# Joined: the experts' last gate and up columns as one product of 512 columns, and attention one's forget gate row among the keys

## The reference

```
s = einsum("bqhd,bkhd->bhqk", qf, kf) * scale                       # 16 heads of 64
s = s + logf_cum[:, :, q0:q1, None] - logf_cum[:, :, None, :q1]     # forget gate, summed over positions
p = softmax(where(mask, s, -inf))

for e in range(8):   # 2816 columns in gate and up
    out = out + gates[..., e:e+1] * (silu(h @ w_gate[e]) * (h @ w_up[e])) @ w_down[e]
```

## Time and profile before

| | |
|---|---|
| median of 3 runs | 1679.54 us (1678.4 to 1681.87) |
| the profiled execution | 1672.49 us |
| its span, first to last instruction | 1670.6 us |
| TensorE busy | 1639.7 us, 98% |
| VectorE busy | 1239.7 us, 74% |
| ScalarE busy | 992.2 us, 59% |
| experts (8 items of some 93.6 us) | about 489 to 1239 us of the span |
| attention one | 405.5 to 444.8 us of the span |

### The profile page before, as it was taken

The page is one execution under the profiler, slowest core; times in us unless marked ns, Lnnn a source line. Parts: engine busy times, 40 slices in busy tenths (PEclk is TensorE's granted clock), DMA queues, the critical chain, the costliest instruction groups (busy, mean ns, idle before and its releaser), DMA issues.

```text
span 1670.6 us, 24525 instructions
## 1 busy us (share of the span) xinstructions
PE 1639.7 (98%) x9456; PEld 1427.2 (85%) x9456; DVE 1239.7 (74%) x1207; ACT 992.2 (59%) x1077; POOL 106.3 (6%) x97
## 2 busy tenths in 40 slices
PE   8999999999999999999999999999999999999998
PEld 6868999898878888888888888888879989979997
DVE  5986544565478988888888898888888478565554
ACT  4245334465457777878787777878774552344443
POOL 1020000000036000000000000000210000000000
PEclk9999999999999999999999999999999999999999
DMA  9405554453059898999989898989994400055450
GB/s 336 154 1 226 190 202 170 158 202 151 25 203 403 312 419 360 391 378 377 422 332 419 332 418 358 395 368 383 373 392 154 152 1 1 8 195 185 175 196 26
DMA packets 53175, 415.17 MB, mean 249 GB/s; under 512 B 6312, under 2 KB 6736, under 8 KB 11888
## 3 DMA queue, kind: packets, MB, share of 16 engines
q1 hardware_dynamic: 49872, 403.65, 61.6%
q0 software_dynamic: 3232, 10.53, 2.0%
HBM read 405.74 MB, written 8.42 MB: 248 GB/s over the span
## 4 chain that ended last, share of the span: by engine, by line
PE 88%; DVE 9%; issue 1%; ACT 1%; DMA 1%; DVEq 0%; SPq 0%; ACTq 0%
PE ps L2040 26%; PE ps L2042 26%; PE ps L2041 26%; DVE big L1816 2%; DVE f L1816 2%; PE ps L2568 1%; PE ps L2376 1%; PE ps L2114 1%; PE ps L2556 1%; DMA ring<-in_ws 1%; PE ps L2495 0%; PE ps L2098 0%; PE ps L2367 0%; PE ps L2128 0%; PE ps L2293 0%
## 5 line engine op out<-in xcount | busy, mean ns | idle before, releaser
L1051 DVE TENSOR_TENSOR wl<-raw,wh 128x2048 fp32r<-128x2048 f32 x194 | 444.3, 2293 | 60.3 <-ACT wh L1046 57.1
L2040 PE MATMUL ps<-wh,f_r 128*128 128x512 f32 (+1 forms) x1216 | 465.3, 383 | 2.0 <-DVE f_r L1782 1.7
L2041 PE MATMUL ps<-wl,f_r 128*128 128x512 f32 (+1 forms) x1216 | 459.8, 378 | 0.0
L2042 PE MATMUL ps<-wh,f_r 128*128 128x512 f32 (+1 forms) x1152 | 435.5, 378 | 0.0
L1046 ACT ACTIVATE wh<-raw 128x2048 fp32r<-128x2048 f32 x192 | 368.3, 1918 | 97.1 <-PE ps L2042 55.0
L2040 PEld LDWEIGHTS ps<-wh,f_r 128*128 128x128 f32 x1216 | 228.8, 188 | 45.0 <-DVE f_r L1782 1.9
L2041 PEld LDWEIGHTS ps<-wl,f_r 128*128 128x128 f32 x1216 | 229.0, 188 | 41.1
L2042 PEld LDWEIGHTS ps<-wh,f_r 128*128 128x128 f32 x1152 | 216.7, 188 | 40.8
L2040 PE MATMUL ps<-ht_t_r,wh 128*128 128x256 f32 x832 | 236.5, 284 | 1.3 <-DVE h_t_r L806 1.0
L2041 PE MATMUL ps<-h_t_r,wh 128*128 128x256 f32 x832 | 235.4, 283 | 0.0
L2042 PE MATMUL ps<-ht_t_r,wl 128*128 128x256 f32 x832 | 235.4, 283 | 0.0
(11 more groups left out here) (446 smaller groups left out, 2137.7 us busy)
## 6 DMA issues: line engine op xcount, KB each, us to landing
raw<-in_ws SPq DMA_DIRECT2D x195, 1024.0 KB, 10.7
raw<-in_ws SPq DMA_DIRECT2D x49, 2048.0 KB, 7.8
big<-in_ws SPq DMA_DIRECT2D x48, 1024.0 KB, 10.9
f<-in_ws SPq DMA_DIRECT2D x24, 1024.0 KB
ring<-in_ws SPq DMA_DIRECT2D x4, 2048.0 KB, 17.9
items<-big SPq DMA_DIRECT2D x8, 512.0 KB, 13.7
gb<-in_gains SPq DMA_DIRECT2D x5, 512.0 KB, 14.2
ring<-in_ws SPq DMA_DIRECT2D x2, 1024.0 KB, 12.8
```

The costliest lines, as they stand in the source:

```text
L1051: nc.vector.tensor_tensor(half_of(wl, h % SPLIT), ring_half(h % HALVES), half_of(wh, h % SPLIT).bitcast(F32), ALU.subtract).then_inc(S("sp ...
L2040: first = nc.tensor.matmul(bank, xh, h, start=start, stop=False)
L2041: nc.tensor.matmul(bank, xh, l, start=False, stop=False)
L2042: return first, nc.tensor.matmul(bank, xl, h, start=False, stop=stop)
```

## The change

**Experts.** The weights of the last step lie on the host as 512 columns, gate's 256 beside up's 256, so a half holds 4 x 512 and not 8 x 256. TensorE makes one product of 512 columns into `ps[1]` from halves 28 and 29, with `transposes(4)` between them. `silu(5)` reads the bank's first 256 columns, `product(5)` multiplies by its last 256. The semaphore `e_gu` counts 11 for an item instead of 12, and ScalarE's `silu(5)` moves behind `tile_t(4)` and half 31.

**Attention one.** The gate's sum becomes one more row of the keys. For an even head the rows 64 to 127 of `KT` are met by zeros in the queries, so row 64 is overwritten by the sum, and the query's row 64 is 1. For an odd head a second copy of the keys, `KTO` (in `g1`), has its own rows 64 to 127 and the sum in row 0, where the odd query has a 1. ScalarE copies the odd keys (four of 64 x 512). GpSimd sets the ones, writes `NL` to a DRAM tensor `decays`, and when this has landed reads it back into the two rows (two DMAs); `g1` is cleared once more after attention. The two matmuls of line 2131, the parts `NLH` and `NLL` and four VectorE instructions that made them are gone, and so is a memset of `NL`.

```diff
@@ gpsimd
             nc.gpsimd.memset(QZS[0], 0.0).then_inc(S("pad"), 1)
+            pool.wait_ge(S("pad"), 3)
+            nc.gpsimd.memset(QZS[0][DH:DH + 1, 0:HEADS:2, :], 1.0).then_inc(S("pad"), 1)
+            nc.gpsimd.memset(QZS[0][0:1, 1:HEADS:2, :], 1.0).then_inc(S("pad"), 1)
+            for n in range(4):
+                b, k = pre.at[("k", n)]
+                pool.wait_ge(pre.free[b], k + 1)
+            pool.wait_ge(S("nl_ready"), 1)
+            pool.dma_start(dr["decays"], NL[0:HEADS, :]).then_inc(S("nl_out"), 16)
+            pool.wait_ge(S("nl_out"), 16)
+            pool.dma_start(KT[DH:DH + 1, :, :], dr["decays"][0:HEADS:2, :].unsqueeze(0)).then_inc(S("nl_rows"), 16)
+            pool.dma_start(KTO[0:1, :, :], dr["decays"][1:HEADS:2, :].unsqueeze(0)).then_inc(S("nl_rows"), 16)
             pool.wait_ge(S("att_done"), 1)
...
+            nc.gpsimd.memset(g1[:, :], 0.0).then_inc(S("pad"), 1)
@@ scalar, keys
             for n in range(4):
                 high_pre(act)
+                b, k = pre.at[("k", n)]
+                act.wait_ge(pre.free[b], k + 1)
+                nc.scalar.activation(KTO[DH:P, 2 * n:2 * n + 2, :], KT[DH:P, 2 * n:2 * n + 2, :], ACT.Copy).then_inc(S("odd_keys"), 1)
@@ scalar, experts
                 high(27, 28, 29, 30)
-                silu(5)
                 tile_t(4)
                 high(31)
+                silu(5)
@@ vector, keys
-            ch(nc.vector.memset(NL, 0.0))
...
-            ch(nc.vector.tensor_tensor_scan(NL[0:HEADS, :], FA[0:HEADS, 3, :], FA[0:HEADS, 1, :], 0.0, ALU.mult, ALU.subtract))
-            ch.go(nc.vector.tensor_copy(NLH[:, 0:SEQ], NL))
-            ch(nc.vector.tensor_copy(NLH[:, SEQ:3 * P], NL[:, 0:P]))
-            nc.vector.tensor_tensor(NLL[:, 0:SEQ], NL, NLH[:, 0:SEQ].bitcast(F32), ALU.subtract).then_inc(S("nl_ready"), 1)
-            nc.vector.tensor_tensor(NLL[:, SEQ:3 * P], NL[:, 0:P], NLH[:, SEQ:3 * P].bitcast(F32), ALU.subtract).then_inc(S("nl_ready"), 1)
+            nc.vector.tensor_tensor_scan(NL[0:HEADS, :], FA[0:HEADS, 3, :], FA[0:HEADS, 1, :], 0.0, ALU.mult,
+                                         ALU.subtract).then_inc(S("nl_ready"), 1)
@@ vector, experts
+                    up = ps[2 + s % 2][:, 0:w] if s < 5 else ps[1][:, w:2 * w]
@@ tensor, attention
-                            pay(nc.tensor.matmul(bank[:, 0:256], qs[:, h, P:2 * P], KT[:, h // 2, 0:256], start=True, stop=False))
-                            nc.tensor.matmul(bank[:, 256:384], qs[:, h, 0:P], KT[:, h // 2, 0:P], start=False, stop=False)
-                            for part in (NLH, NLL):
-                                nc.tensor.matmul(bank[:, 0:384], IDA[:, h:h + 1].to_broadcast([P, P]), part, start=False, stop=False)
+                            keys = (KT, KTO)[h % 2]
+                            pay(nc.tensor.matmul(bank[:, 0:256], qs[:, h, P:2 * P], keys[:, h // 2, 0:256], start=True, stop=False))
+                            nc.tensor.matmul(bank[:, 256:384], qs[:, h, 0:P], keys[:, h // 2, 0:P], start=False, stop=False)
...
-            pe.wait_ge(S("nl_ready"), 2)
+            pe.wait_ge(S("odd_keys"), 4)
+            pe.wait_ge(S("nl_rows"), 32)
@@ tensor, experts
                 for s in range(6):
-                    product(ps[s % 2], 512 if s < 5 else 256)
-                    if s:
-                        transposes(s - 1)
-                    product(ps[2 + s % 2], 512 if s < 5 else 256)
                     if s == 5:
+                        product(ps[1], lambda: transposes(4))
                         rows(0)
                         rows(1)
                         down_step(4, lambda: transposes(5))
-                    elif s:
+                        continue
+                    product(ps[s % 2])
+                    if s:
+                        transposes(s - 1)
+                    product(ps[2 + s % 2])
+                    if s:
                         down_step(s - 1)
```

More of the change, by code:

```diff
@@ L424, in build @@
         IDA, CAU = big_r[:, 2816:2816 + P], big_r[:, 2816 + P:2816 + 2 * P]
-        NLH, NLL = big_r[:, 3072:3072 + 3 * P], big_r[:, 3072 + 3 * P:3072 + 6 * P]
         SUMS = rt[:, 96:128].rearrange("p (t h) -> p t h", t=TT)
         FA = big[:, 1792:1792 + 4 * SEQ].rearrange("p (b s) -> p b s", b=4)
-        KT = f1[:, :].rearrange("p (c s) -> p c s", s=SEQ)
+        KT, KTO = (t[:, :].rearrange("p (c s) -> p c s", s=SEQ) for t in (f1, g1))
         HKBS = [t[:, 1024:2048].rearrange("p (h s) -> p h s", s=SEQ) for t in (f1, f3)]
@@ L1090, in delta_act @@
         def delta_act(act, ch):
-            act.wait_ge(S("pad"), 6)
+            act.wait_ge(S("pad"), 9)
             for n in range(6):
@@ L1261, in _ @@
             norm_act(act, pre, 2, "x_done", 2, [("mix1", HTQ), ("kv", HTK)])
-            act.wait_ge(S("pad"), 3)
+            act.wait_ge(S("pad"), 5)
             high_pre(act)
@@ L1299, in _ @@
             act.wait_ge(S("routed"), 1)
-            act.wait_ge(S("pad"), 5)
+            act.wait_ge(S("pad"), 7)
             act.sem_inc(S("y_out"), 1)
@@ L1306, in silu @@
                     w = 512 if s < 5 else 256
-                    act.wait_ge(S("e_gu"), i * 12 + (2 * s + 1))
+                    act.wait_ge(S("e_gu"), i * 11 + (2 * s + 1))
                     nc.scalar.activation(SG[:, s % 2, 0:w], ps[s % 2][:, 0:w], ACT.Silu).then_inc(S("e_silu"), 1)
@@ L1593, in delta_dve @@
             bank2 = filled(dve, post, ("gT",))
-            dve.wait_ge(S("pad"), 7)
+            dve.wait_ge(S("pad"), 10)
             ch(nc.vector.tensor_copy(GTR, bank2[0:GH, 0:SEQ]))
@@ L1921, in product @@
                     w = 512 if s < 5 else 256
-                    dve.wait_ge(S("e_gu"), i * 12 + (2 * s + 2))
+                    dve.wait_ge(S("e_gu"), i * 11 + min(2 * s + 2, 11))
                     dve.wait_ge(S("e_silu"), i * 6 + (s + 1))
-                    nc.vector.tensor_tensor(PRD[:, s % 2, 0:w], ps[2 + s % 2][:, 0:w], SG[:, s % 2, 0:w],
+                    up = ps[2 + s % 2][:, 0:w] if s < 5 else ps[1][:, w:2 * w]
+                    nc.vector.tensor_tensor(PRD[:, s % 2, 0:w], up, SG[:, s % 2, 0:w],
                                             ALU.mult).then_inc(S("e_prod"), 1)
@@ L2329, in _ @@
             gather(1, None, 2)
-            pe.wait_ge(S("pad"), 5)
+            pe.wait_ge(S("pad"), 7)
             for n in range(4):
@@ L2345, in half_unit, with product @@
                     return half_of(wh, h % SPLIT), half_of(wl, h % SPLIT)
-                def product(bank, n):
-                    per = HALF // n
+                def product(bank, between=None):
+                    n, per = 512, HALF // 512
                     for part in range(DC // per):
+                        if part and between:
+                            between()
                         h, l = (t.rearrange("p (c n) -> p c n", c=per) for t in half_unit())
@@ L2731, in lay_out @@
             else:
-                put(g[:, :, sl], u[:, :, sl])
+                put(np.concatenate([g[:, :, sl], u[:, :, sl]], axis=2))
             if s:
@@ L2785 @@
     dr["scratch"] = nc.dram_tensor("scratch", (GH, HK), F32).ap()
+    dr["decays"] = nc.dram_tensor("decays", (HEADS, SEQ), F32).ap()
     dr["tokens"] = nc.dram_tensor("tokens", (SEQ, D), F32).ap()
```

## The result

The changed kernel takes **1671.3 us** (median of 20 runs, 1665.85 to 1675.03) against 1675.23 for the kernel before on the same chip (20 runs, 1671.61 to 1681.87). The ratio is 0.9969, interval 0.9956 to 0.9982: 0.31% faster, some 5.2 us. That is the distance of the two means. The medians lie only 3.9 us apart, but each list falls into two groups (before: ten runs up to 1673.8 and ten from 1676.7 on), so a median stands in a gap or at its edge and is the looser figure. The three runs of before shown ahead lay high with their 1679.54. The spans of the profiled executions are 1670.6 and 1665.8 us, 4.8 apart.

The account below looks back on a forecast made before the run. TensorE was taken as the bound, nearly gapless in experts and attention one. The experts' 2.4 us plus attention's 3.6 make 6.0 off 1679.54, giving 1673.5 us (ratio 0.9964), range 1669.5 to 1678 us.

Parts of the forecast that it names:

- A pair of matmuls for one is worth 12.5 ns, the step 2.4 us: Experts' last step: 24 wide matmuls replace 48 narrow, 0.30 us an item, 2.4 us over 8 items.
- The rival that wide ones gain nothing: Experts' step: a wide matmul gains almost nothing over two narrow, leaving 3.6 us, 1675.9 us; chance 0.05.
- the 0.5 us by the gap that the Trainium skill gives: Experts' step: by a gap of N/2.4 + 2.5 ns a pair is worth 2.5 ns, the step 0.5 us.
- The later silu costs nothing, a slack of 0.25 stays: Experts' tail: nothing on VectorE waits for `silu(5)`; slack before the last down step falls from 0.40 to 0.25 us.
- The rival of the stalled tail: Experts' tail: the later silu delays VectorE's chain by 0.55 us or more, leaving 3.6, 1675.9 us; chance 0.13.
- 0.35 us a head, heads of 1.77: Attention one: dropping two 384-column matmuls a head saves 0.35 us, 5.6 over 16; heads some 1.77 us up to head 8.
- The first exponentials take back 0.7: Attention's start: three pairs go but ScalarE's answer comes only one pair earlier, so 0.7 us is lost.
- 0.8 and 0.5 are lost in heads 8 to 15, since VectorE is nearly full: Attention: 0.8 us lost from head 8's maxima to head 9's values, 0.5 in heads 13 to 15; 3.6 us left.
- New waits at heads 9, 11 and 13, under 1 us: Attention, next profile: TensorE newly waits for VectorE's copies of these odd heads, under 1 us each.
- The rows cost nothing: GpSimd's two DMA trips, 3 us each, end at 397, ahead of attention at 405.47; slack 8 us.
- The warning about VectorE and GpSimd's descriptors: Rows' DMAs: VectorE can delay GpSimd's descriptor writing, some 0.6 us becoming 3.1; 2.5 more a trip stays inside the slack.
- Everything after each stage only shifts: Whole kernel: work behind the changed stages keeps its length, so the 6.0 us comes off the total.

Follow-up runs that it names:

- e13_later: The changed kernel with VectorE's low part of four finished heads one head later (heads 9, 13, 17 instead of 8, 12, 16); 1666.31 us, one run.
- e5_quarters: The changed kernel with VectorE's two quarters of a weight half moved from behind heads 8 and 10 to behind heads 7 and 13; ratio to before 0.9958.
- e3_again: The changed kernel run once more, unaltered, for a second profile; 1671.14 us, ratio to before 0.9967.
- e6_table: The changed kernel with ScalarE's table of exponentials loaded ahead of attention; 1667.81 us, ratio to before 0.9951.
- e1_attention: The changed kernel with the experts' edits undone, leaving attention's half alone; 1673.08 us, ratio to before 0.9971.
- e8_trips: The changed kernel with the gate's sum written to DRAM seven times instead of once, one behind the other, ahead of the reads; 1672.43 us, one run.
- the fill: Matmuls of no use added in TensorE's last two waits of attention; on the changed kernel alone 1670.54 us, ratio to before 0.9964.

## Why the prediction was right, and where it was not

The time came out inside the range and near the forecast: 6.0 us were predicted, 5.2 measured (4.8 between the two spans). That the absolute time came out so near is in part luck. It lies 2.2 under mine: the base, three high runs, was 4.3 above the later median of before, and the medians' gain of 3.9 was 2.1 short of 6.0, so two errors partly cancel. By its steps:

- *A pair of matmuls for one is worth 12.5 ns, the step 2.4 us.* Right: 5.92 us where I said 5.9, 2.33 over the loop, 2.25 alone. The rival that wide ones gain nothing is out, and so are the 0.5 us by the gap that the Trainium skill gives (TensorE: Matmul & The Clock Gate, Back-to-back issue gap).
- *The later silu costs nothing, a slack of 0.25 stays.* Right; it is 0.37, and no wait stands in the loop. The rival of the stalled tail is out.
- *0.35 us a head, heads of 1.77.* Right.
- *The first exponentials take back 0.7.* Right: the wait grew from 0.82 to 1.51. What it hides I had not looked for: 1.28 of it is a table load beside an idle ScalarE.
- *0.8 and 0.5 are lost in heads 8 to 15, since VectorE is nearly full.* Right in the main. 3.6 was expected for the stage, 3.72 measured. From head 8's maxima to head 9's values it is now 428.33 - 419.81 = 8.52 us, where it was 431.18 - 422.12 = 9.06: 0.54 shorter, within the 0.45 to 0.73 that the prediction gave. By the distances between the heads' scores, and against 0.35 a pair, 0.87 us are lost between heads 10 and 13 and 0.30 behind, 1.17 in all for the 1.3. `e13_later` bears the reason out for head 9: with only the order changed its wait stays (0.64), behind a VectorE that was busy nearly without a gap from 422.02 on. That less work there would shorten it is not shown, since `e5_quarters` put another wait ahead. What the prediction had not seen is the other kind of loss, an instruction that waits for ScalarE with a copy behind it. That is the 1 us at the end of the heads; it is in both kernels, so the difference between them does not show it.
- *New waits at heads 9, 11 and 13, under 1 us.* Two of the three came, 0.46 and 0.28; the one of 1.00 was there before.
- *The rows cost nothing.* Right: last landing 396.0 where I said 397, slack 9.6. The warning about VectorE and GpSimd's descriptors (the Trainium skill, SBUF — State Buffer, "SBUF: two separate sides") has no counterpart in these rows: the issues took 0.50 to 0.52 us and the first trip landed after 1.7. But the Trainium skill speaks there of VectorE copying from SBUF to SBUF, and here VectorE was idle at the first issue and ran a subtraction at the other two, so this is no test of it.
- *Everything after each stage only shifts.* This sentence failed. Behind the heads TensorE ran at 1.2 GHz for some 3.4 us, +1.56. That is more than the 1.2 by which the spans' 4.8 fall short of 6.0; most of the rest is 0.4 us gained behind the experts, which no step foresaw (430.6 to 430.7 in six profiles with attention's edit, 430.9 and 431.0 without it) and no run explains. The clock fell there in four of the seven profiles with attention's edit and no fill (after, `e3_again`, `e5_quarters`, `e6_table`; not `e1_attention`, `e8_trips`, `e13_later`), in neither of the two without the edit, and in none of the five with the fill.

Open: whether the edit causes that fall behind attention. The two waits of 1.00 us in the tail stand in before as well, and 4 of 7 against 0 of 2 settles nothing. Open too is whether the fill lengthens the router's fall. All five filled kernels have a long one in their profile (47.4 to 48.9 us from the last transposes to the experts, 2.8 to 4.3 over the 44.6 of `e1_attention`), and of the nine others only `e3_again` has; but among timed runs of like clock the filled ones do not stand above the rest (36 runs: 1667.8 and 1672.2 at high and low clock, of which 15 at the high one). That ScalarE could take over VectorE's copies of heads 9 and 11 was not tried.

## What to carry to other kernels

When an engine seems to hold up a late result, ask two questions apart: how much work it has between its start and that result, and which instruction in its queue waits for a third engine, with what behind it. Here the first explains the wait at head 9's values and the second the one at the end of the heads: moving one call by one head gave 1.18 us, 0.93 of it at the end, and moving real work from steps 8 and 10, in the first of which it filled a wait, to steps 7 and 13 lost 1.14. Look at where a gain arises, too; the stage of `e13_later` came out near the expectation for another reason. Two small products with the same stationary operands are worth joining for the fixed part alone, and can be priced to the tenth of a microsecond from distances between starts. Where a gain of a few microseconds is at stake, cut the span into stages and read the granted clock in each before believing a total: here one stage that nobody touched takes from 44.6 to 50.6 us.

## What the hardware showed that I had not expected

- The granted clock falls to 1.2 GHz during 32 matmuls of 8 columns (12 of 14 profiles) or up to 4.4 us behind them, for 7 to 20.5 us, though TensorE's rows show it busy: in the changed kernel 1.00 of 1.00 us in 470 to 471, and the fall at 471.2. That these matmuls cause it is not shown; no run has the router without them. The Trainium skill, TensorE: Matmul & The Clock Gate, "Part 1: The HAM clock gate", says that the monitor's windows run free of the kernel's start, so that the same kernel is slowed by different amounts; the executions of one kernel, 46.18 and 50.61 us for the same stage, agree with that.
- With idle places of TensorE filled, the clock stayed up behind them (five of five, against three of the seven unfilled ones with attention's edit), and the total gained nothing that the times show.
- An 8 KB read into one partition landed after 1.8 and 2.4 us on quiet DMA engines, and after 4.1 while their share rose from 0.48 to 0.99.
- GpSimd's memset of `g1` took 1.82 us behind attention, where nobody waited.
